# The mixer projections of a two-layer backbone as three rounded matmuls, on a smaller weight ring

## The reference

```python
for l in range(2):
    sh1, sc1, g1, sh2, sc2, g2 = silu(c) @ ada_w[l] + ada_b[l]      # c for latents, c_ctx for context
    h = rms_norm(x, norm1_w[l]) * (1 + sc1) + sh1
    p_rw, p_ret, p_hg, p_gate = split(h @ w_in[l], (1920, 2048, 2560, 3072))
    y_rw, v_first = rwkv7_mixer(p_rw, h, v_first, ...)   # layer 1 also takes h @ v_down (32 columns)
    y_ret = retention_mixer(p_ret, ...)                  # q, k, v, gate of 512 columns each, 4 heads
    y_hg = hgrn2_mixer(p_hg, ...)                        # q, two forget gates, input, gate, 4 heads
    merged = sum(sigmoid(gate_b) * (y_b @ w_branch[l, b]) for b in 3 branches)
    x = x + g1 * (merged @ w_out[l])
    h2 = rms_norm(x, norm2_w[l]) * (1 + sc2) + sh2
    x = x + g2 * (square(relu(h2 @ mlp_w1[l])) @ mlp_w2[l])         # 4096 hidden columns
out = rms_norm(x[latents], final_norm_w)
```

## Time and profile before

| | us |
|---|---|
| median of 3 runs | 2741.78 |
| the profiled execution | 2744.85 |
| its span | 2743.1 |
| granted clock of TensorE over the span | 0.943 |
| PE busy | 2462.0 |
| DVE, ACT, POOL busy | 1178.4, 923.2, 437.1 |

### The profile page before, as it was taken

How to read it: one execution, slowest core, us unless ns; L and a number is a source line. 1 busy time by engine, 2 the same in 40 slices (tenths; PEclk the granted TensorE clock), 3 DMA queues, 4 the chain that set the end, 5 groups by cost and what they waited for, 6 DMA issues and landing times.

```text
span 2743.1 us, 54656 instructions
## 1 busy us (share of the span) xinstructions
PE 2462.0 (90%) x23538; PEld 1856.9 (68%) x23538; DVE 1178.4 (43%) x1831; ACT 923.2 (34%) x1308; POOL 437.1 (16%) x455
## 2 busy tenths in 40 slices
PE   4988989898999889998999989888879898898998
PEld 1553748494855568876888856466857766598998
DVE  2323444444423343445444433254453523366665
ACT  3323232223234332334223342332232334345554
POOL 0002221212123310001000000132231314400000
PEclk8999999899999989998999989999989999899999
DMA  7313322313011023332233232200000012055553
GB/s 277 126 51 117 133 73 77 115 35 147 3 62 54 35 85 96 100 123 70 92 97 95 92 125 77 71 18 25 3 24 10 18 44 73 35 177 196 157 179 103
DMA packets 64031, 239.38 MB, mean 87 GB/s; under 512 B 7088, under 2 KB 8240, under 8 KB 62512
## 3 DMA queue, kind: packets, MB, share of 16 engines
q1 hardware_dynamic: 61920, 218.13, 24.0%
q10 hardware_dynamic: 1872, 17.75, 1.6%
HBM read 230.62 MB, written 5.24 MB: 86 GB/s over the span
## 4 chain that ended last, share of the span: by engine, by line
PE 79%; DVE 8%; ACT 6%; POOL 3%; issue 2%; DMA 2%; ACTq 0%; DVEq 0%; SPq 0%; POOLq 0%
PE psum L411 13%; PE psum L384 11%; PE psum L386 11%; PE psum L385 11%; PE psum L398 10%; PE psum L758 7%; PE psum L420 2%; PE psum L762 2%; PE psum L483 2%; PE psum L720 2%; PE psum L658 1%; POOL work L1799 1%; ACT L1383 1%; PE psum L447 1%; DMA work<-in_ret_constants 1%
## 5 line engine op out<-in xcount | busy, mean ns | idle before, releaser
L398 PE MATMUL psum<-normed,weight_ring 128*128 128x512 f32 (+1 forms) x864 | 372.5, 589 | 33.4 <-ACT normed L1437 12.6
L398 PEld LDWEIGHTS psum<-normed,weight_ring 128*128 128x128 f32 x864 | 176.5, 209 | 225.8 <-issue 210.2
L411 PE MATMUL psum<-work 64*64 64x64 f32 (+1 forms) x9088 | 307.7, 222 | 14.9 <-ACT work L1618 10.5
L929 DVE TENSOR_TENSOR weight_ring_parts<-weight_ring,weights_high 128x1024 fp32r<-128x1024 f32 (+1 forms) x224 | 266.7, 1191 | 125.5 <-ACT weights_high L1398 121.1
L411 PEld LDWEIGHTS psum<-work 64*64 64x64 f32 x9088 | 294.7, 135 | 26.6 <-issue 15.6
L385 PE MATMUL psum<-normed_low_part,weights_high 128*128 128x512 f32 (+1 forms) x896 | 304.1, 339 | 0.0
L1398 ACT ACTIVATE weights_high<-weight_ring 128x1024 fp32r<-128x1024 f32 (+1 forms) x224 | 230.8, 1030 | 160.5 <-PE psum L386 149.0
L758 PE MATMUL psum<-normed,weight_ring 128*128 128x512 f32 (+1 forms) x512 | 200.6, 539 | 2.7 <-ACT work L1383 2.7
L384 PE MATMUL psum<-normed_high,weights_high 128*128 128x512 f32 (+1 forms) x512 | 178.3, 348 | 15.6 <-DVE normed_low_part L917 15.2
L385 PEld LDWEIGHTS psum<-normed_low_part,weights_high 128*128 128x128 f32 x896 | 173.3, 193 | 21.3 <-issue 0.5
L386 PE MATMUL psum<-normed_high,weight_ring_parts 128*128 128x512 f32 (+1 forms) x512 | 176.9, 346 | 0.0
(11 more groups left out here) (241 smaller groups left out, 4218.6 us busy)
## 6 DMA issues: line engine op xcount, KB each, us to landing
weight_ring<-in_weights SPq DMA_DIRECT2D x406, 512.0 KB, 3.6
x_scratch<-work ACTq DMA_DIRECT2D x2, 2048.0 KB, 7.4
weight_ring<-in_weights SPq DMA_DIRECT2D x16, 256.0 KB, 2.8
work<-x_scratch ACTq DMA_DIRECT2D x2, 2048.0 KB, 10.3
work<-in_ret_constants ACTq DMA_DIRECT2D x2, 1152.0 KB, 12.7
work<-in_small_weights ACTq DMA_DIRECT2D x2, 1152.0 KB, 5.2
work<-in_x ACTq DMA_DIRECT2D x1, 2048.0 KB, 14.8
constants<-in_constants ACTq DMA_DIRECT2D x1, 1315.0 KB, 9.1
```

Source lines behind the costliest of these rows:

```text
L398: last = mm(ps[:, 0:t1 - t0], tiled(s, k), hT[:, k, t0:t1], start=(k == 0), stop=(k == KT - 1))
L411: last = mm(ps[q, w * m:w * m + w], lhs(q, m), rhs(q, m), start=True, stop=True)
L929: tt(ring_r[:, i % RING, o], ring[:, i % RING, o], high[:, n % HIGHS, o].bitcast(F32), ALU.subtract).then_inc(vec_split.sem, vec_split.ste ...
```

## The change

- RING 9 becomes 6, HIGHS 4 becomes 3, and ACT and DVE run 3 slots ahead in place of 4.
- All projections of the mixers are `rounded` products: retention, small, RWKV, HGRN. `v_down` becomes a fourth small slot, padded to 128 columns, in layer 1. That puts 51 slots of layer 0 and 52 of layer 1 more through `weights_high` and `weights_low`.
- `normed_high` gets a place of its own; POOL casts the 8 tiles after norm 1 and norm 2, DVE's `normed_low` follows two tiles behind. The casts and subtractions of the gates' input (`gate_input_high`, `gate_input_low`) are gone.
- Retention values of all four heads are computed first, from 4 slots that each hold two k-tiles of 512 columns (`tokens_out`), in the 4 dense banks; ACT drains them after the last. HGRN's input goes through the same function.
- The projections and the norm sum of retention, and those of HGRN, move from the big to the dense banks. A bank's wait is now found from what last held it in any pool (`held`).
- Modulation rows are spread one at a time: after rk of heads 0 to 2, at kk, values, level 1 and level 3 of each RWKV c, and the last one after the gates of f = 0.
- The keys of a HGRN level move into the place of `v_first`, which is saved to DRAM before HGRN of layer 0 and read back after it.
- In layer 0 ACT splits the first three slots before norm 1. DVE splits the values' first two slots before the norm's tail, the other two and the first two projections after it, then computes the strips, then splits head 0's third projection.

The core of the diff; in "..." stand the same edits of waits (a loop over `freed()`), the host's layout and the repeats:

```diff
-RING = 9
-HIGHS = 4
+RING = 6
+HIGHS = 3
...
+    ("start", 0): [(0, 0), (0, 1), (0, 2), (0, 3), None],
+    ("rk", 0, 0): [(0, 4)], ("rk", 0, 1): [(0, 5)], ("rk", 0, 2): [(0, 6)],
+    ("kk", 0, 0): [(0, 7)], ("values", 0, 0): [(0, 8)], ("level1", 0, 0): [(0, 9)], ("level3", 0, 0): [(0, 10)],
...
+def mixer_order(l):
+    out = [("rv", l, q) for q in range(4)]
+    out += [("ret", l, c, j) for c in range(NT) for j in range(3)]
+    out += [("small", l, j) for j in range(3 if l == 0 else 4)]
+    out += [("rw", l, c, j) for c in range(NT) for j in (1, 0, 2)]
+    out += [("hf", l, h, j) for h in range(4) for j in range(4)]
+    return out + [("hi", l, q) for q in range(4)]
...
-        key_mix = nc.alloc_sbuf_tensor_at("keys_of_a_level", [P, 2, 2, N], F32, offset=place["weights_high"])
+        normed_hi = sb("normed_high", [P, KT, N], F32R)
+        key_mix = nc.alloc_sbuf_tensor_at("keys_of_a_level", [P, 2, 2, N], F32, offset=place["v_first"])
...  (PE)
+            def project(pool, filled, w, key, t0=0, tiles=range(KT)):
+                if 0 in tiles:
+                    pool.fill(*key)
+                    for free in pool.freed():
+                        eng.wait_ge(*free)
+                ps = pool.get(*key)[:, 0:N - t0]
+                for k in tiles:
+                    last = rounded(ps, w, (normed_hi[:, k, t0:N], hT_r[:, k, t0:N]), k, k == 0, k == KT - 1)
...
+            def tokens_out(name, w, l, q, tiles, after_norm=False):
+                for i in tiles:
...
+                    for k in (2 * q, 2 * q + 1):
+                        if after_norm and i == 0:
+                            eng.wait_ge(vec_mlp.sem, vec_mlp.at("normed split", l, 1, k))
+                        c = slice(BW * (k % 2), BW * (k % 2) + BW)
+                        mm(ps, normed_hi[:, k, t], w[0][:, c], start=(k == 0), stop=False)
+                        mm(ps, normed_hi[:, k, t], w[1][:, c], start=False, stop=False)
+                        last = mm(ps, hT_r[:, k, t], w[0][:, c], start=False, stop=(k == KT - 1))
...
+                for q in range(4):
+                    tokens_out("rv", split("rv", l, q), l, q, range(4), True)
                 for what, c in ret_order:
...
                     if what == "P":
+                        project(dense, dense_filled, split("ret", l, c, 0), ("rq", l, c), lo)
+                        project(dense, dense_filled, split("ret", l, c, 1), ("rk", l, c))
+                        modulation("rk", l, c)
+                        project(dense, dense_filled, split("ret", l, c, 2), ("rg", l, c), lo)
...  (DVE)
+                weights_low(split_at["rv", l, 2])
                 tail(l, 1)
+                weights_low(split_at["ret", l, 0, 1] + 1)
                 for h in range(4):      # the strips, as before
...
+                    if what == "P":
+                        weights_low(split_at["ret", l, c, 2] + 1)
+                        modulation("rk", l, c)
                     if what == "R":
...
+                            weights_low(split_at["ret", l, c, i] + HIGHS + 1)
...
+                    weights_low(split_at["rw", l, c, 2] + 3)
...
-                        weights_low(split_at["m1", l, f] + AHEAD + 1)
+                        weights_low(split_at["m1", l, f] + HIGHS)
...  (ACT)
                 modulation("start", l)
+                if l == 0:
+                    weights_high(HIGHS)
                 norm(l, 1)
...
+                weights_high(split_at["ret", l, 0, 1] + 1)
+                eng.wait_ge(dense_filled.sem, dense_filled.at("rv", l, 3))
+                for i in range(4):
+                    act(wk(RT_V + 512 * i), dense.get("rv tile", l, i), ACT.Copy).then_inc(...)
...
                         if c == 0:      # after rk was drained: the 16 exponentials, as before
...
+                        modulation("rk", l, c)
...
-                        weights_high(split_at["m1", l, f] + AHEAD + 1)
+                        weights_high(split_at["m1", l, f] + HIGHS)
```

More of the change, by code:

```diff
@@ L517, in _ @@
                         eng.wait_ge(pool_ret.sem, pool_ret.at("ret squared", l, c))
-                        sum_over(ones, wk(RT_O + 512)[:, lo:N], ("rN", l, c), w)
-                for j in range(3):
-                    project(slot("small", l, j), ("small", l, j), lo if j == 2 else 0, N)
+                        tile_sum(wk(RT_O + 512)[:, lo:N], ("rN", l, c), w)
+                for j in range(3 if l == 0 else 4):
+                    project(big, big_filled, split("small", l, j), ("small", l, j), lo if j == 2 else 0)
                 eng.wait_ge(loaded_small_weights.sem, loaded_small_weights.at("small weights", l))
-                if l > 0:
-                    ps = big.fill("vd", l)
-                    eng.wait_ge(*big.freed())
-                    for k in range(KT):
-                        last = mm(ps[0:32, :], work[:, RW_W + 1536 + 32 * k:RW_W + 1536 + 32 * k + 32], hT[:, k, :],
-                                  start=(k == 0), stop=(k == KT - 1))
-                    last.then_inc(big_filled.sem, big_filled.step(("vd", l)))
-                modulation("small", l)
                 def low_rank(c, d):
@@ L1020, in _ @@
                     A = RT_A + 1536 * (c % 2)
-                    if what == "P" and c == 0:
-                        modulation("strips", l)
+                    if what == "P":
+                        weights_low(split_at["ret", l, c, 2] + 1)
+                        modulation("rk", l, c)
                     if what == "R":
@@ L1162, in _ @@
                     modulation("kk", l, c)
-                    modulation("keys", l, c)
                     for d in range(2):
@@ L1182, in _ @@
                         eng.wait_ge(vec_rwkv.sem, vec_rwkv.n)
+                    modulation("values", l, c)
                     for d in range(2):
@@ L1440, in norm @@
                 act_norm.also(("h", l, which))
+                if which == 2:
+                    weights_high(split_at["out", l, KT - 1] + HIGHS + 1)
             rows = []
@@ L1891, in _ @@
                     before = slots[i - RING]
-                    done = mid_filled if before[0] == "ada" else dense_filled if before in split_at else big_filled
+                    done = filled_by(before)
                     eng.wait_ge(done.sem, done.at(*last_use(before)))
```

397 lines of the change are left out of this document (213 added, 184 removed), and 7 rows, old and new, of the table ADA_AT.

## The result

The changed kernel takes 2771.4 us (median; 2769.7 to 2773.2), the kernel before 2741.4 beside it: ratio 1.0113, 95% interval 1.0093 to 1.0132. One of the four runs of the kernel before, 3275.7 us, was slow as a whole, and the ratio leaves it out. The forecast was 2684 with a range of 2640 to 2730. It is **wrong in sign**, and 87 us off. The span of the profiled execution went from 2743.1 to 2767.9, +24.8, where the sum had -57.4: a miss of 82.

What follows compares the result with a forecast made beforehand. TensorE (PE), busy 90% of the span, was taken as the bound. Stage terms summed to -57.4 on the profiled 2744.85, giving 2687.4, or 2684 for the median; range 2640 to 2730 (8 in 10).

Steps and rivals of the forecast that it cites:

- Matmuls: Rounded projections, both layers: 5.54 us wide instead of 6.87, 2.80 narrow, 125 us saved in all; at the skill's spacing 150.
- rival D: Rounded products no faster in these stages, because of extra waits for weight loads; called nearly excluded, chance 0.10 together with C.
- Head: Before norm 1: +13 (12.6) from row waits on the shorter ring, ACT's three splits and casts; first squares near 47.
- Retention: Layer 0 +10.9, with 22 for the wait at the strips (PE gap near 17 behind rk); layer 1 -4.8.
- Small projections: Layer 0's small stage: -11, as two modulation rows and their wait go, less 3.4 for the third projection's uncovered way.
- RWKV of layer 0: -22, 5.5 per c: 11 gained before the first keys product, projections 1.33 and 1.9 faster, rows paid later; DVE splits free.
- Three rows of 2.9 are paid later: RWKV of layer 0: in each c three modulation rows move between levels, at 2.9 us each.
- rival B: DVE and POOL become the chain: 103 more splits cost 31 to 62 us, 2715 to 2745; chance 0.18.
- HGRN: -19.4 in layer 0, -12.7 in layer 1, after adding back a third of a us per slot for late ACT splits.
- the turn: From HGRN to the gates: 5 us less in layer 0, 6 in layer 1, as casts and subtractions go; bounds 0 and 8.
- Dense stages of layer 1: Merge, out and MLP: +11 from three high parts, 4.8 at m1 slots and 6 at gates and branches; bounds 0 and 30.
- C: Fewer buffers pace the dense stages, 121 slots per layer; at 0.5 us each 2794, slower; chance 0.10 together with rival D.

Runs made afterwards that it cites:

- Run 3: The kernel before with a ring of six slots, the row of "out" moved behind ga's first three slots and one split less ahead: ratio 1.0207, 2803.5 us.
- run 5: The changed kernel with 15 modulation rows taken out of layer 0's retention and RWKV and put ahead of norm 1: 2835.2 us in one run.
- Runs 1: The changed kernel with layer 0's twelve RWKV rows at values, level1 and level3 loading 8 columns per slot, not 1024, their matmuls reading a constant: ratio 1.0042.
- run 14: run 13 with six added 2 MB memory-to-memory bursts that nothing waits for, in the levels of layer 0's first three RWKV c: ratio 0.9857.
- 15: The changed kernel with loads of layer 0's rows at kk, values, level1 and level3 of RWKV cut to 8 columns, matmuls reading a constant: 2758.1 us, one run.
- run 6: The changed kernel with ACT's weight split in HGRN held back behind the copies of the next level's keys: ratio 0.9997.
- run 2: The kernel before with three high parts and a lead of three slots (HIGHS 3, AHEAD 2), nothing else: ratio 1.0066.
- Run 10: The changed kernel with the weight splits of merge and MLP ahead of the drains, still with three high parts: ratio 1.0078.
- run 13: The changed kernel with strips by head, HGRN splits behind key copies, layer 1's rows in layer 0's MLP, kk row pairs, merge splits ahead of drains: 0.9772, 2681.0 us.
- run 7: The changed kernel with layer 1's twelve modulation rows moved into layer 0's MLP, one behind a slot of m1: ratio 1.0014.

## Why the prediction was wrong, step by step

**Matmuls, right.** A wide projection takes 5.44 to 5.65 us in the changed kernel, against 5.54 forecast; rival D is excluded. Only behind a pause it takes 6.4 to 8.2. (The prediction's aside on a still faster matmul adds up to some 155 us, not 150; nothing else uses it.)

**Head, nearly right**, +15.4 for +12.6. Run 3 gives 14.1 to the ring. The first squares start at 51.14 where "near 47" was the sign, so the rows and splits ahead of them were put 4 too low, and the casts behind the squares add 0.8 instead of 2.

**Retention, half right.** The wait at the strips was seen in its place: 20.57 in layer 0, with 0.88 before, and 18.09 in layer 1. In layer 1 it has the size of the sum (12.6 + 5.5). In layer 0 "near 17" was the sign, and the 3.7 more are the ring: ACT waits 4.33 for a slot's DMA ahead of the strips. In run 5, with no row there, that DMA wait is gone and PE's is 18.09; with the row, row and wait take 22.5, 4.4 more. The sum had 2 for the ring. (It also took 22 where its own terms give 18.8 - 1.9 + 5 - 0.9 = 21.) The 6.6 in layer 1 I can't divide.

**Small projections, right**, -14.3 for -11. PE waits 3.59 ahead of the low rank products, where 3.4 was put, though by its own terms (8 less 5.5) it would be 2.5.

**RWKV of layer 0, the step that failed**: forecast 4 x -5.5, measured +23.6. I cut each c at DVE's first keys product. Its distance from the low rank product, in the four c: before 43.5, 45.0, 49.0, 43.9, after 36.4, 34.9, 34.8, 35.0. What lies behind it: before 80.3, 81.7, 81.4, 73.2, after 98.6, 95.2, 94.1, 92.4.
- *"11 us gained"* was read from the third c, which has the longest pause of the four: 11.3, where the others have 9.4, 9.0 and 6.2. And *"projection 1 gives 1.33, projection 0 1.9"* were counted as if PE set this stretch. DVE sets it once the pause is gone (PE then waits for DVE's keys, 18.5 and 12.3 us in all). The gain was 40.3 instead of 56.9: 17 of the miss.
- *"Three rows of 2.9 are paid later"*: 12 rows cost 53.5 by run 5, not 35: 18 or 19 of the miss. Runs 1, 14 and 15 show a reason: without the loads of all 16 rows the stage is 15.6 shorter, 2 MB bursts stop PE for up to 2.7 us at a time, and the clock falls to 0.89 behind such a gap. The sum priced a row by its matmuls alone and put nothing for its loads.
- The wait ahead of HGRN's first product, 6.12 where it was 1.26: 5. The sum put nothing for it. By the order of the fills, worked out from the kernel, this product now takes PSUM bank 0, which holds the gate's product of the last c until DVE has used it (L1294, the releaser in the row); before, it took the other bank of the big pool and waited for ACT. No run tests another bank.
- *The 12 splits on DVE "cost nothing there"*: right within 1 us per c (run 5). This was rival B's ground, and B as put forward fails in this stage.

That is 41 of 46; the rest is spread over what lies behind the first keys product, and is no more than this stage differs between two profiles.

**HGRN, right mechanism, wrong size; the turn, wrong.** "A third of a us late on each of 16" was 5.4 in layer 0 and 6.6 in layer 1; run 6 gives 8.6 and 11.2, 0.54 and 0.70 per slot. The split isn't only late itself: it stands ahead of a copy of 0.42 that PE's next level waits for. The turn to the gates was to give 5 and 6, since the casts that stood ahead of POOL's square are gone. It gave 2.8 and 0.2: PE's waits there are 5.34 and 1.87 in layer 0, where they were 7.13 and 2.85, and in layer 1 5.45 where it was 5.63. So the casts were not most of this wait; what is, stays open. The two together make 5.4 us in layer 0, where the miss is 5.0, and 10.4 in layer 1, where it is 12.4.

**Dense stages of layer 1**: forecast +11, measured +19.1. The mechanism, three high parts, was right (run 2: 18.9 alone), the place wrong: m1 was to pay 4.8, and the MLP paid 6.6; the merge, 6 forecast, paid 12.5, of which PE waits 11.3 in nine places for DVE's split. Run 10 gets 10 of it back by order. (The 4.8 is 0.15 for 32 slots; the 28 written there would give 4.2.) Layer 0 was right: a slot of 5.54 covers it.

**Rivals.** None had the sign with the right cause. C, slower, put the loss at the dense stages: they took 8 of the 82. Its 121 slots per layer are 112 (x224 in the earlier trace rows), which moves its 2794 to 2785 and changes nothing else. The loss lay in moved work whose neighbours had no room, and it could be won back: run 13 has the same products and buffers and takes 2681. That this is 3 us from the forecast's 2684 is chance, as run 13 is another kernel. Nor does it show that the rounded products gave 2.3%: run 13 also moves rows into the MLP and spreads the strips, and no run gives the kernel before the same moves.

## What to carry to other kernels

When work is moved out of a block that has become too long, what is gained is the pause that it caused at each place, read at every repetition, and only down to the next engine's own chain; price it where it goes by a row from that kind of stage. Put loads and their products into a stage of wide matmuls, with other work between a row and its columns (3.0 us per row in the MLP), not between chains of small ones (4.5). Where an engine makes both a part for later and a copy that the next product needs, the copy goes first.

## What the runs showed of the hardware

A burst of 2 MB of loads stops PE in a stage of 64-column matmuls, though PE waits for none of its bytes: up to 2.7 us at a time, 15.4 us in 10 places over the four c with six such bursts in run 14, 0.9 us in 3 places in run 13, which has them not, 18.3 in 12 places in the changed kernel and 0.8 in 2 in the kernel before. The windows above show it: with DMA at 297 GB/s PE is still full (6.98 of 7.00 us); directly after, it works for 2.39 of 4.80. In the MLP of layer 0, into which run 7 puts twelve such bursts, PE has no such idle time at all.

The start times of the packets in the instruction queue, 16 KB each, tell what the pauses are. In the changed kernel one such packet starts at 337.64 and the next only at 347.25, behind 2.1 MB of weights, and PE goes on at 349.61. All ten pauses of more than 1 us there end 2.2 to 2.5 us after such a packet starts, with 1.6 to 2.1 MB moved since the packet before; the seven of run 14 end 2.3 to 2.6 us after one. A moment picked at random in this stage stands so in 7 of 100. In run 5, where rows stand only at kk, these packets start 4.4 us apart in the median. So PE stands still for want of instructions that come late behind the burst, as far as times can show it; which engine a packet is for, the trace doesn't say.

The Trainium skill ("Runtime: NRT & Kernel Launch", "Instruction fetch mechanics") says that an engine's sequencer fetches its instructions through a DMA queue of its own in blocks of 256, one ahead of the work, and calls the cost of crossing a block mostly hidden. The trace agrees without the six bursts among the small products (0.9 us of such idle time over four c in run 13), and does not with them (15.4 us in run 14).
